# Gate and up projections channel-major from the second group of a SwiGLU, w_down still by token

## The reference

```python
def swiglu(h, w_gu, w_down):
    gu = jnp.einsum('bsd,df->bsf', h, w_gu)
    g, u = jnp.split(gu, 2, axis=-1)
    return jnp.einsum('bsf,fd->bsd', jax.nn.silu(g) * u, w_down)
...
        x = x + g1 * token_mixer(h, ...)
        h = rms_norm(x, norm2[l]) * (1.0 + sc2) + sh2
        x = x + g2 * swiglu(h, w_gu[l], w_down[l])
```

## Time and profile before

| | |
|---|---|
| device time, median of 3 | 975.89 us (974.9 to 978.88) |
| the profiled execution: its own time | 971.84 us |
| its span | 969.6 us |
| mean granted TensorE clock | 0.993 |
| PE busy | 913.4 us |
| DVE busy | 708.9 us |
| ACT busy | 499.6 us |

### The profile page before, as it was taken

One profiled execution on the slowest core, in us unless ns is written; L12 is line 12 of the kernel. 1 busy time (PEld: TensorE's weight loads), 2 busy tenths in 40 slices (PEclk: granted clock), 3 DMA queues, 4 the chain that ended last, 5 costly groups with the idle time before them and its releaser, 6 DMA issues.

```text
span 969.6 us, 12842 instructions
## 1 busy us (share of the span) xinstructions
PE 913.4 (94%) x5020; PEld 779.2 (80%) x5020; DVE 708.9 (73%) x1145; ACT 499.6 (52%) x738; POOL 29.4 (3%) x53
## 2 busy tenths in 40 slices
PE   8998979998997999999989998899989889999998
PEld 5887969976975788888868997898679668888886
DVE  5987889787787667585675788988878856565454
ACT  6455775455447343443573478374453754343441
POOL 1010000000000000000010000000000000000000
PEclk9999999999999999999999999999999999999999
DMA  9978723414652757775466884251445345645441
GB/s 377 410 305 365 249 88 131 174 44 174 261 204 100 272 208 272 285 280 202 150 241 210 303 320 155 88 205 56 173 170 223 138 150 196 244 152 205 173 174 44
DMA packets 29581, 198.12 MB, mean 204 GB/s; under 512 B 3281, under 2 KB 3793, under 8 KB 7506
## 3 DMA queue, kind: packets, MB, share of 16 engines
q1 hardware_dynamic: 23474, 155.22, 42.8%
q0 software_dynamic: 5760, 41.95, 11.5%
q10 hardware_dynamic: 288, 0.14, 0.1%
HBM read 196.24 MB, written 1.05 MB: 203 GB/s over the span
## 4 chain that ended last, share of the span: by engine, by line
PE 55%; DVE 28%; ACT 8%; issue 5%; DMA 3%; DVEq 0%; ACTq 0%
PE bank L566 13%; PE bank L567 13%; PE bank L568 13%; DVE w_lo L1315 9%; PE bank L527 3%; PE bank L529 3%; PE bank L528 3%; ACT w_hi L965 3%; DMA raw<-in_slabs_dram 3%; DVE front L1322 3%; DVE acc L1622 2%; DVE score L1531 2%; DVE score L1549 1%; PE bank L902 1%; DVE acc L1322 1%
## 5 line engine op out<-in xcount | busy, mean ns | idle before, releaser
L1315 DVE TENSOR_TENSOR w_lo<-raw,w_hi 128x2048 fp32r<-128x2048 f32 (+2 forms) x146 | 316.3, 2172 | 111.2 <-ACT w_hi L965 109.2
L965 ACT ACTIVATE w_hi<-raw 128x2048 fp32r<-128x2048 f32 (+2 forms) x146 | 262.8, 1806 | 96.5 <-PE bank L568 65.1
L566 PE MATMUL bank<-w_hi,h_hi 128*128 128x512 f32 x536 | 214.1, 400 | 10.4 <-DVE w_lo L1315 7.3
L567 PE MATMUL bank<-w_hi,h_lo 128*128 128x512 f32 x536 | 210.6, 393 | 0.0
L568 PE MATMUL bank<-w_lo,h_hi 128*128 128x512 f32 x536 | 210.4, 393 | 0.0
L566 PEld LDWEIGHTS bank<-w_hi,h_hi 128*128 128x128 f32 x536 | 101.5, 189 | 36.1 <-issue 7.9
L568 PEld LDWEIGHTS bank<-w_lo,h_hi 128*128 128x128 f32 x536 | 101.5, 189 | 22.1
L567 PEld LDWEIGHTS bank<-w_hi,h_lo 128*128 128x128 f32 x536 | 101.4, 189 | 19.9
L527 PE MATMUL bank<-h_hi,w_hi 128*128 128x256 f32 x384 | 111.5, 290 | 5.7 <-DVE w_lo L1315 5.7
L528 PE MATMUL bank<-h_lo,w_hi 128*128 128x256 f32 x384 | 108.6, 283 | 0.0
L529 PE MATMUL bank<-h_hi,w_lo 128*128 128x256 f32 x384 | 108.6, 283 | 0.0
(11 more groups left out here) (206 smaller groups left out, 1399.9 us busy)
## 6 DMA issues: line engine op xcount, KB each, us to landing
raw<-in_slabs_dram SPq DMA_DIRECT2D x124, 1024.0 KB, 4.8
front<-in_ada_dram POOLq DMA_DIRECT2D x31, 1024.0 KB, 5.7
acc<-in_ada_dram POOLq DMA_DIRECT2D x9, 1024.0 KB, 8.1
raw<-in_slabs_dram SPq DMA_DIRECT2D x16, 552.0 KB, 5.0
front<-in_ada_dram SPq DMA_DIRECT2D x5, 1024.0 KB, 10.7
raw<-in_slabs_dram SPq DMA_DIRECT2D x6, 768.0 KB, 5.9
proj<-in_ada_dram SPq DMA_DIRECT2D x2, 1024.0 KB, 8.6
x_t<-in_x_dram SPq DMA_DIRECT2D x2, 512.0 KB, 4.4
```

Of the source, the lines that this page charges most:

```text
L566: nc.tensor.matmul(o, hh, wh, start=first, stop=False)
L567: nc.tensor.matmul(o, hl, wh, start=False, stop=False)
L965: nc.scalar.activation(w_hi[:, n % RING, 0:w], raw[:, n % RING, 0:w], ACT.Copy).then_inc(hi_ready.sem, 1)
L1315: nc.vector.tensor_tensor(w_lo[:, n % RING, 0:w], raw[:, n % RING, 0:w], w_hi[:, n % RING, 0:w], ALU.subtract).then_inc(lo_ready.sem, 1)
```

## The change

From group 1 on, gate and up are computed channel-major, 48 matmuls of 256 columns for a slab, into banks 4 and 5 (even groups) or 6 and 7 (odd groups), all 256 tokens at once. The product then already has channels on the partitions: it is rounded straight from SBUF and not transposed, and silu, product, rounding and low part are one instruction of 128 x 512 each for a group. Group 0 stays token-major, with its four transposes after the first slab of group 1, to bank 0. `w_down` stays token-major. Both halves of the gate row are transposed in group 7, to banks 4 and 5. On ACT, `hi(gu_slab(1, 0))` moves ahead of the second token tile's `norm_finish`, and in the last group `hi(down_slab(10))` comes after silu and `glu_high`. On DVE the adaLN sums stay last in a group, and `lo(down_slab(10))` comes after the product. The diff, cut to its core:

```diff
-        silu_g = [proj[:, 0, 256 * i:256 * (i + 1)] for i in range(2)]
-        glu = [proj[:, 1, 256 * i:256 * (i + 1)] for i in range(2)]
+        silu_g = [proj[:, 0, 512 * i:512 * (i + 1)] for i in range(2)]
+        glu = [proj[:, 1, 512 * i:512 * (i + 1)] for i in range(2)]
...
+                def turn_glu():
+
+                    pe.wait_ge(glu_done.sem, glu_done.at(l, 2))
+                    for t in range(TT):
+                        for f in range(2):
+                            last = nc.tensor.transpose(bank[0][:, f * T + t * P:f * T + (t + 1) * P],
+                                                       glu[0][:, 256 * t + f * P:256 * t + (f + 1) * P], ident)
                     last.then_inc(glu_tp.sem, 1)
+
+                def gate_up(i, kg):
+
+                    par = i % 2
+                    slot = slab(l, gu_slab(i, kg))
+                    if kg == 0 and i >= 2:
+                        pe.wait_ge(glu_done.sem, glu_done.at(l, i))
+                    hi, lo = [h_hi[:, 4 * kg + k, :] for k in range(4)], [h_lo[:, 4 * kg + k, :] for k in range(4)]
+                    channel_slab(slot, [(bank[4 + 2 * par + e][:, m * T:(m + 1) * T], 256 * e + m * P,
+                                         [512 * k for k in range(4)], hi, lo, m == 0)
+                                        for e in range(2) for m in range(2)],
+                                 kg == 0, kg == 1).then_inc(slab_used.sem, 1)
...
-                for i in range(FG):
-                    gate_up(i, 0, 0)
-                    if i == 1:
-                        turn_glu(0, 1)
-                    gate_up(i, 0, 1)
-                    gate_up(i, 1, 0)
-                    turn_glu(i, 0)
-                    if i in (6, 7):
-
-                        if i == 7:
-                            pe.wait_ge(row_out.sem, row_out.at(l, 3))
-                        turn_row(l, 1, i - 6, bank[7])
-                    gate_up(i, 1, 1)
-                    if i == 0:
-                        continue
+                for t in range(TT):
+                    for kg in range(2):
+                        gate_up_first(t, kg)
+                for i in range(1, FG):
+                    gate_up(i, 0)
+                    if i == 1:
+                        turn_glu()
+                    if i == 7:
+
+                        pe.wait_ge(glu_done.sem, glu_done.at(l, 8))
+                        for half in range(2):
+                            turn_row(l, 1, half, bank[4 + half])
+                    gate_up(i, 1)
+                    if i == 7:
+                        pe.wait_ge(row_out.sem, row_out.at(l, 4))
                     down(i - 1, 0)
                     if i == FG - 1:
 
-                        turn_glu(i, 1)
                         down(i, 0)
-                    else:
-                        turn_glu(i, 1)
                     down(i - 1, 1)
...
                 norm_by_token(l, 1, 1)
+                hi(l, gu_slab(1, 0))
                 norm_finish(l, 1, 1)
-                hi(l, gu_slab(1, 0))
                 table(ACT.Silu)
...
+                silu_first(0)
+                hi(l, gu_slab(1, 1))
+                silu_first(1)
+                glu_high(0)
+                for i in range(1, FG):
+                    hi(l, down_slab(i - 1))
                     if i + 1 < FG:
                         hi(l, gu_slab(i + 1, 0))
+                    silu(i)
+                    glu_high(i)
+                    if i == 7:
+                        for half in range(2):
+                            row_copy(l, 2 + half, bank[4 + half])
+                    if i + 1 < FG:
+                        hi(l, gu_slab(i + 1, 1))
                     else:
                         hi(l, down_slab(i))
-                    silu(i, 1)
-                    if i + 1 < FG:
-                        hi(l, gu_slab(i + 1, 1))
-                    elif l + 1 < DEPTH:
-                        hi(l + 1, S_A)
-                    glu_high(i, 1)
+                        if l + 1 < DEPTH:
+                            hi(l + 1, S_A)
...
+                glu_first(0)
+                lo(l, gu_slab(1, 1))
+                glu_first(1)
+                glu_low(0)
+                ada_step(0)
+                for i in range(1, FG):
+                    lo(l, down_slab(i - 1))
                     if i + 1 < FG:
                         lo(l, gu_slab(i + 1, 0))
+                    glu_step(i)
+                    glu_low(i)
+                    if i + 1 < FG:
+                        lo(l, gu_slab(i + 1, 1))
+                        ada_step(i)
                     else:
                         lo(l, down_slab(i))
```

More of the change, by code:

```diff
@@ L394, in build @@
         xd_done = event("xd_done", 3)
[L395 to L400, removed]
+        gu_done = event("gu_done", 1)
+        silu_done = event("silu_done", FG + 1)
+        glu_done = event("glu_done", FG + 1)
+        glu_tp = event("glu_tp", 1)
+        glu_hi_done = event("glu_hi_done", FG)
+        glu_lo_done = event("glu_lo_done", FG)
         dve_chain = event("dve_chain", 0)
@@ L876, in _, with gate_up_first @@
                 w_out(3, 1, (2, 3)).then_inc(slab_used.sem, 1)
[L878 to L882, removed]
+                def gate_up_first(t, kg):
+                    slot = slab(l, gu_slab(0, kg))
                     for kk in range(4):
                         k = 4 * kg + kk
-                        if i == 0 and k % 2 == 0:
+                        if k % 2 == 0:
                             pe.wait_ge(nlo_done.sem, nlo_done.at(norm_no(l, 1), 4 * t + k // 2 + 1))
-                        if i == 0 and t == 0 and k == 6:
+                        if t == 0 and k == 6:
                             for half in range(2):
@@ L1246, in _, with silu_first @@
                 norm_by_token(l, 1, 1)
+                hi(l, gu_slab(1, 0))
                 norm_finish(l, 1, 1)
-                hi(l, gu_slab(1, 0))
                 table(ACT.Silu)
-                def silu(i, t):
-                    n = 2 * i + t
+                def silu_first(t):
                     if t == 0:
-                        act.wait_ge(gu_done.sem, gu_done.at(l, i + 1))
+                        act.wait_ge(gu_done.sem, gu_done.at(l, 1))
                     else:
[L1257 to L1272, removed]
-                    if i == 0:
[L1274 to L1279, removed]
+                        act.wait_ge(slab_used.sem, slab_used.at(l, gu_slab(0, 1) + 1))
@@ new lines, in silu_first, with silu, glu_high @@
+                    nc.scalar.activation(silu_g[0][:, 256 * t:256 * (t + 1)], bank[4 + t][:, 0:256], ACT.Silu)\
+                        .then_inc(silu_done.sem, 1)
+                def silu(i):
+                    act.wait_ge(slab_used.sem, slab_used.at(l, gu_slab(i, 1) + 1))
+                    nc.scalar.activation(silu_g[i % 2], bank[4 + 2 * (i % 2)][:, :], ACT.Silu).then_inc(silu_done.sem, 1)
+                def glu_high(i):
+                    if i == 0:
+                        act.wait_ge(glu_tp.sem, glu_tp.at(l, 1))
+                    else:
+                        act.wait_ge(glu_done.sem, glu_done.at(l, i + 2))
+                    nc.scalar.activation(glu_hi[i % 2][:, :, :].rearrange("p f t -> p (f t)"),
+                                         glu[i % 2] if i else bank[0][:, :], ACT.Copy).then_inc(glu_hi_done.sem, 1)
@@ L1697, in _, with glu_first, glu_step, glu_low @@
                 lo(l, gu_slab(1, 0))
[L1699 to L1704, removed]
-                        .then_inc(glu_done.sem, 1)
[L1707 to L1711, removed]
+                def glu_first(t):
+                    dve.wait_ge(silu_done.sem, silu_done.at(l, t + 1))
+                    at = slice(256 * t, 256 * (t + 1))
+                    nc.vector.tensor_tensor(glu[0][:, at], silu_g[0][:, at], bank[4 + t][:, 256:512], ALU.mult)\
+                        .then_inc(glu_done.sem, 1)
+                def glu_step(i):
+                    dve.wait_ge(silu_done.sem, silu_done.at(l, i + 2))
+                    nc.vector.tensor_tensor(glu[i % 2], silu_g[i % 2], bank[5 + 2 * (i % 2)][:, :], ALU.mult)\
+                        .then_inc(glu_done.sem, 1)
+                def glu_low(i):
+                    dve.wait_ge(glu_hi_done.sem, glu_hi_done.at(l, i + 1))
+                    nc.vector.tensor_tensor(glu_lo[i % 2][:, :, :].rearrange("p f t -> p (f t)"),
+                                            glu[i % 2] if i else bank[0][:, :],
+                                            glu_hi[i % 2][:, :, :].rearrange("p f t -> p (f t)"), ALU.subtract)\
                         .then_inc(glu_lo_done.sem, 1)
@@ L1718, in ada_step @@
                         ada_next()
[L1720 to L1730, removed]
+                glu_first(0)
[5 more added lines that the diff above has]
+                    lo(l, down_slab(i - 1))
                     if i + 1 < FG:
                         lo(l, gu_slab(i + 1, 0))
+                    glu_step(i)
```

(3 more changed lines are left out.)

9 lines of the change are left out of this document (1 added, 8 removed).

## The result

The changed kernel takes 986.16 us (median of 4 runs, 984.49 to 988.13), the kernel before 975.39 (4 runs, 971.61 to 978.88): ratio 1.0126, 95% interval 1.0103 to 1.0149. It is slower by 1.3% by this ratio, by 1.1% (10.8 us) from median to median, and 3.1 us above the forecast of 983.1. The profiled execution took 984.49 (span 982.2), 12.6 us of span more than the one of before.

What follows compares the result with a forecast made beforehand. The PE, busy 94% of the span, was taken as the bound. Terms -11.1 + 1.4 + 6.6 + 7.1 + 3.2 = +7.2 us take the median from 975.89 to 983.1, range 977.5 to 989.

Steps and rivals of the forecast that it cites:

- The first group: Group 0 without transposes in it, rounding moved: group 2 starts 5.6 us earlier in layer 0, 5.5 in layer 1; -11.1.
- the late slab: Layer 0: group 0's down slab is rounded later, so down waits until 321.1 instead of 320.6; 0.5 us.
- The steady groups: Nine groups per layer, 256-column matmuls for 512-column ones and transposes: each 0.08 us longer; +1.4, from -2.0 to +2.5.
- The last group: The last down slab, rounded after `glu_high(10)`, comes late: PE idle 3.55 us in each layer; +7.1.
- rival B: 256-column matmuls in long rows cost 0.1135 us each: total -4.0, 971.9, not slower; chance 0.04.
- Group 7: PE waits in front of down of group 6 for ACT's two row copies: idle 3.3 us per layer; +6.6.
- Rival C: The chains behind the waits in group 7 and the last group are hidden, half their price, no falls: 973.0; chance 0.08.
- The clock: After four new idles of 3.3 to 3.6 us, two falls to the 1.2 GHz level at 1.6 each; +3.2.
- Rival A: The clock keeps its 2.4 GHz through all four new idles: +4.0, 979.9, within 0.5%; chance 0.22.
- rival D: The clock falls after all four new idles: +10.4, 986.3; chance 0.10.
- Rival E: DVE's adaLN sums make `lo(down_slab)` late in six more groups of layer 0, 0.5 each: adds 3, 986; chance 0.06.

Runs made afterwards that it cites:

- e10_token_mended: `e6_token_group0` with silu and product of group 1's first tile ahead of rounding group 0's down slab, adaLN sums one group later: 961.42 us against 974.48, ratio 0.9856.
- e4_rounding_only: The kernel before with only the rounding `hi(gu_slab(1, 0))` moved ahead of `norm_finish`: 967.66 us against 973.68, ratio 0.9940.
- e5_no_move: The changed kernel with the moved rounding put back behind `norm_finish`: 987.19 us against 974.92 for the kernel before, ratio 1.0142.
- e1_row_wait_later: The changed kernel with the wait for the row copies moved from down of group 6 to the start of group 8: 976.13 us against 974.92, ratio 1.0024.
- e2_last_slab_early: The changed kernel with the last down slab rounded ahead of the last silu on ACT, likewise on DVE: 975.94 us against 974.92, ratio 1.0017.
- e8_down_order: The changed kernel with the second half of down 9 queued ahead of the first of down 10: 978.13 us against 973.68, ratio 1.0040.
- e12_fill_last: The changed kernel plus 12 unused 512-column matmuls where the PE waits in the last group: 984.07 us against 974.48 for the kernel before, ratio 1.0089.
- e6_token_group0: The kernel before, token-major everywhere, with the rounding moved and group 0's transposes set back into group 1: 969.96 us against 973.68, ratio 0.9963.

## Why the prediction was right, by its own steps

Its mechanisms and its sign came true; one term was mis-sized, the clock.

**The first group** was put at -11.1 and gave -11.3, net of the 0.5 lost in layer 0 to the late slab, as the prediction had it. That the gain comes from the order of work is shown: `e10_token_mended` has it all with token-major groups. The moved rounding by itself is worth 6 us in the old form and 1 us in the new (`e4_rounding_only`, `e5_no_move`).

**The steady groups** were put at +0.08 each and are +0.10: 96 matmuls in 11.51 us are 0.1199 each, the upper of the two rows that the prediction stood between the earlier trace rows. The eight distances from group 2 to group 10 are 0.91 longer in each layer. The last group, which the prediction took to be like the others, differs: in the kernel before, its second pair of transposes stands behind the first half of down (482.90). So up to its down it is 0.33 longer, and 0.2 of that come back behind it. Together +2.1 instead of +1.4. The 0.1135 of rival B did not appear. Nor did the 0.109 that the Trainium skill gives in TensorE: Matmul & The Clock Gate, section Back-to-back issue gap, for a matmul of 256 columns.

**Group 7** was put at 3.3 for each layer and gave 3.20: the two row copies took 1.06 together, not 1.2. **The last group** was put at 3.55 and gave 3.6. Each vanishes under its own edit (`e1_row_wait_later`, `e2_last_slab_early`) while the other stays, and for both the order of work on ACT is the cause. Rival C (hidden chains) is out.

**The clock** was put at two falls of 1.6, +3.2. Three of the four possible falls came, within the "one to three" that the forecast stood for, but one was longer than its price: down took 7.22 and 7.01 instead of 5.58 in group 7 (+1.6 and +1.4), and behind the idle of layer 0's last group 13 matmuls took 5.65 where 3.03 would do (+2.6). That is +5.7. Rival A (no fall) is out, and on this term rival D (four falls, +6.4) is nearer than the forecast. That falls of the longer kind exist no rival had.

With these sizes the sum is -11.3 + 2.1 + 6.4 + 7.2 + 5.7 = +10.1, and the forecast of +7.2 lacks 2.9: 2.5 for the clock and 0.7 for the steady groups, less 0.3 for the rest. Set on the forecast's 983.1 this gives 986.0, where 986.16 was measured. The remaining 2.5 of the 12.6 lie in the mixer, whose code the change doesn't touch. They belong to this pair of profiled executions: that of the kernel before took 971.84, 3.5 us less than the median of 975.39, and it kept its clock after the 3.23 us idle in front of 93, as only three of the thirteen profiles did. The medians are 10.8 apart, close to the sum without the mixer. That the total came within 3.1 us is in part luck, since how many falls an execution has is chance, as the last section shows.

**Rival E** (more late slabs in groups 2 to 6) is out: the timeline has no wait for `w_lo` there.

## What to carry to other kernels

When work is regrouped into fewer, larger pieces on the engines that follow the PE, every wait of the old order has to be asked again: which instruction now stands ahead of the one awaited, and what is queued behind the wait. Here the layout itself cost 2.1 us, and two waits at places where the regrouped work ends late cost 19, though moving either takes a few lines. Where a gain is found with a change of layout, try it with the order alone: here the old layout with the new order was the fastest.

## What was not expected of the hardware

In 16 places a dense stream of matmuls stood for 3.0 to 3.4 us behind gate and up of group 7 or inside the last group. In 13 the 1.2 GHz level followed. L marks a slow stretch about twice as long as the others:

| profile | group 7, layer 0 | group 7, layer 1 | last, layer 0 | last, layer 1 |
|---|---|---|---|---|
| the changed kernel | fell | fell | fell, L | kept |
| `e1_row_wait_later` | | | fell, L | fell |
| `e2_last_slab_early` | fell, L | fell | | |
| `e5_no_move` | fell | kept | fell | fell, L |
| `e8_down_order` | kept | fell | | |
| `e12_fill_last` | fell | fell | | |

The idle of 3.10 in `e6_token_group0` was followed by slow clock too. The same instruction fell in one profile and not in another (904.61 in `e2_last_slab_early` did, 911.36 in `e5_no_move` did not), and the idle of 3.1 to 3.2 in front of 93 in the mixer, at equal code, fell in ten of the thirteen profiles. So a fall differs from execution to execution, but it is a likely one, and even odds were too low for it. The single row that the prediction had against a fall, 93.45 in the kernel before, was one of the rare ones. Nor does the length of the idle alone order the cases: in the mixer idles of 2.76 to 2.79 (126.16 in the kernel before, and its like) fell in 24 of 25 cases, more often than the longer ones. The Trainium skill has, in TensorE: Matmul & The Clock Gate, section "HAM oscillation — how this bites in real kernels", that waits of some 3 to 5 us between bursts of matmuls make the next burst start cold; 13 of the 16 cases agree, three do not.

A slow stretch in dense work costs 1.4 to 1.7 us in nine of the 13 cases and 2.6 to 2.7 in four. The one from 487 to 494 is of the long kind, and the PE was busy again from 488.12. What decides the length, no run here shows. At 13 of 16 and these prices an idle of this kind costs some 1.5 us more than itself, where the prediction had taken 0.8 (an estimate from these cases).

A spacing of 0.1199 for weight load and 256 columns held over all groups of channel-major work, against 0.2269 for 512 columns in the gate and up matmuls: twice the instructions cost 5.7% more time, with the PE called busy in both.
